# Rotating the three SBUF places of the FFN weight units in a hybrid decoder layer on eight cores

## The chip, the cores and the metric

The kernel runs on the eight cores of one Trainium2 chip. Every core takes half of the tokens of one of the four sequences, so all run the same program on data of their own. The metric is the device time of the slowest core, in microseconds (us). Engine names: PE is TensorE, DVE is VectorE, ACT is ScalarE, POOL is GpSimd, SP is SyncE.

## The reference

One decoder layer over `x` of 4 x 2048 x 2048 in float32. RMSNorm and one input projection feed two head groups: a causal pooling mixer and sparse attention with a compressed, a selected and a sliding-window branch. Their outputs pass an output projection and are added to `x`. Then follow the two steps that matter here, and a last RMSNorm:

```python
h = h + swiglu(rmsnorm(h, ffn_norm_g[i]), w_gate[i], w_up[i], w_down[i])
gate = jax.nn.sigmoid((rmsnorm(h, ple_norm_g[i]) @ w_ple_gate[i]).astype(jnp.float32)).astype(h.dtype)
h = h + (p[i] @ w_ple_proj[i]) * gate
...
def swiglu(x, w_gate, w_up, w_down):
    return (jax.nn.silu(x @ w_gate) * (x @ w_up)) @ w_down
```

The hidden width of the FFN is 5632, that is 44 chunks of 128.

## The kernel before, in words

**Order of the work.** The program is written as a list of operations, each with the buffers that it reads and writes (class `Sched`). Two buffers whose byte ranges in SBUF overlap depend on each other: the first use of the later one waits for all readers of the earlier one (`buf`, `_touch`, lines 54 to 83). A planner (`order`, lines 174 to 277) then plays the list through with a cost per operation and writes down, for each engine, the order in which its operations start. On the chip each engine runs its list in that order and waits on semaphores, so a wait holds up all that stands behind it on that engine. Of operations that are ready at the same planned time, the one that comes first in the program goes first. For DMAs the planner assumes 290e3 bytes per us (line 135), shared evenly by the bytes of a piece between the SP queue and the POOL queue when both hold work (`flow`, lines 207 to 229), each queue being first in, first out, with a start 1.2 us after its issue (line 264) and 0.55 us from landing to the reader (line 246).

**FFN.** Each core holds 1024 tokens as two halves of 512 (called half 0 and half 1). The 44 chunks are done in three groups of 16, 16 and 12 (`NQ_FF`, line 351). Gate and up weights come in *units* of 256 columns. The first pair of units is multiplied plainly (`plain_pair`); all others by a scheme with seven products of eight matmuls each instead of eight (`seven`, lines 191 to 227), for which DVE first forms sums of weight quarters (`weight_sums`, line 134). A unit needs 8 KB per partition for its weights and three sums of 2 KB. Three places take turns: unit `u` of the list `SEQ` uses place `u % 3` (lines 1129 to 1142). The down weights of the first two groups go through the same places as units 16 to 23 and 40 to 47. `SEQ` has 60 units; the last group is units 48 to 59, so unit 57 is in place 0, unit 58 (the last gate) in place 1, and unit 59 (the last up) in place 2.

**The last group's down projection.** Its down weights are eight tiles `wdn` of 6 KB each (line 1335), all in bytes of their own:

```python
wdn = [tile(f"wdl{i}", (R1 + 12 * KB, R1 + 18 * KB, R5 + 28 * KB, R5 + 34 * KB, R5, R5 + 6 * KB, R1, R1 + 6 * KB)[i], [12, 256], BF16) for i in range(8)]
...
    in_turn(latest + [load_dn(WD_FIRST[gi - 1])])
...
late = [load_dn(dmc) for dmc in range(2, 6)]
```

They are used in the order 6, 7, 0, 1, 2, 3, 4, 5 (`DM_LAST`, line 1330). Tiles 6, 7, 0 and 1 are loaded while the last group runs (line 1354). Tiles 2 to 5 (`late`, line 1358) lie in the region at `R5` where the units' places are, and so wait for units. Each load is three DMAs on the POOL queue that cast float32 to bfloat16. The embedding input `pT` (line 1360, two DMAs) lies at `AH` and waits for the unit that had that place. The first two gate weights of the next stage, `wpg0` and `wpg1`, come behind them (line 1378).

At the same time SP reads the residual stream back from HBM (`y_mid`) in 18 loads of 512 KB in one fixed order (lines 1367 to 1376). For most of half 1 it lies in two pieces, which DVE adds on arrival (line 1375, six additions of 1024 columns).

The products themselves are 32 tiles of 12 matmuls (lines 1381 to 1388), 16 for half 0 and then 16 for half 1. PSUM has 8 banks and the tiles take them in turn (`bank`), tile `k` and tile `k + 8` the same one; behind the first tile of half 1 the norm of half 0 takes a bank as well, which shifts the later ones by one. DVE adds each tile to the residual (`add_h`, line 963), and that frees the bank. The adds of L543 belong to the norm's statistics. Behind it comes the gate of the layer embedding (`ple`, line 1428; its own matmuls are L455 and L1440).

**At the start of the FFN**, units 0 to 2 are loaded into the places as soon as the output projection is done with the weights `wo` that lie there (lines 1156 and 1157).

The lines that the change touches, and those that use them:

```python
1108 UNITS = [([R5, R5 + 8 * KB, R5 + 10 * KB, R5 + 12 * KB]), [R5 + 14 * KB, R5 + 22 * KB, R5 + 24 * KB, R5 + 26 * KB], [R5 + 28 * KB, R5 + 36 * KB, R5 + 38 * KB, AH]]
1110 for i, o in enumerate(UNITS):
1111     w_ = view(o[0], [2, 8, 2, 128], BF16)
1112     B = S.buf(f"uw{i}", o[0], 8 * KB)
1113     units.append((w_, B, [tile(f"ut{i}{k}", o[1 + k], [8, 128], BF16) for k in range(3)]))
...
1131         w_, B, _ = units[u % 3]
1132         latest[:] = [load("pool", f"uw{u % 3}", w_.rearrange("p a b c d -> p (a b c d)"), SEQ[u], B)]
```

Of the kernel before, what the change touches and what calls it, by code (L numbers as in the profile page):

```python
# [15 lines left out]
KB = 1024  # L16
# [329 lines left out]
R4, R5, R6 = int(116.5 * KB), int(148.5 * KB), int(188.5 * KB)  # L346
# [6 lines left out]
def build():  # L353
# [43 lines left out]
    def view(off, shape, dtype=F32):  # L397
        n = int(np.prod(shape)) * (2 if dtype == BF16 else 4)
        assert off % 4 == 0 and n % 4 == 0 and off + n <= ARENA_BYTES, (off, shape)
        ap = arena[0:128, off // 4:(off + n) // 4]  # L400
        if dtype == BF16:
            ap = ap.bitcast(BF16)
        if len(shape) > 1:
            names = "abcd"[:len(shape)]
            kw = {names[i]: shape[i] for i in range(len(shape) - 1)}
            ap = ap.rearrange(f"p ({' '.join(names)}) -> p {' '.join(names)}", **kw)
        return ap
# [71 lines left out]
    AH = SCR + 12 * KB  # L479
# [625 lines left out]
        for q in range(4):  # L1105
            S.dma("sp", lambda e, q=q: e.dma_start(out=h_d[:, 4 * q:4 * q + 4, h, :], in_=hT[h][:, 4 * q:4 * q + 4, :]), f"hs{h}{q}", B_h[h][4 * q:4 * q + 4], [B_hd_of[4 * q + k][h] for k in range(4)])

    UNITS = [([R5, R5 + 8 * KB, R5 + 10 * KB, R5 + 12 * KB]), [R5 + 14 * KB, R5 + 22 * KB, R5 + 24 * KB, R5 + 26 * KB], [R5 + 28 * KB, R5 + 36 * KB, R5 + 38 * KB, AH]]
    units = []
    for i, o in enumerate(UNITS):  # L1110
        w_ = view(o[0], [2, 8, 2, 128], BF16)
# [526 lines left out]
```

How the kernel before makes its waits and increments, by code:

```python
        def run(e, engobj):  # L309
            waited = {}
            for o in ops[e]:
                need = {}
                for d in o.deps:
                    if d.dma_key is None:
                        sem, val, key = esem[d.eng], d.sigval, ("e", d.eng)
                    else:
                        sem, val, key = dsem[d.dma_key], d.dma_val, ("d", d.dma_key)
                    if need.get(key, (None, -1))[1] < val:
                        need[key] = (sem, val)
                for key, (sem, val) in need.items():
                    if waited.get(key, -1) >= val:
                        continue
                    waited[key] = val
                    engobj.wait_ge(sem, val)
                ins = o.fn(engobj)
                if o.dma_key is not None:
                    ins.then_inc(dsem[o.dma_key], 16)
                    for fn in o.more:
                        fn(engobj).then_inc(dsem[o.dma_key], 16)
                elif o.signal:
                    ins.then_inc(esem[e], 1)
```

## Time and profile before

| what | us |
|---|---|
| median of 3 runs | 1563.32 |
| lowest of the 3 runs | 1561.86 |
| the profiled execution's own time | 1561.98 |
| its span on the slowest core (core 1) | 1560.4 |
| spans of the eight cores | 1552.2 to 1560.4 |
| PE busy on core 1 | 1510.2 |

The span is from a core's first instruction to its last one. The execution's own time holds 1.6 us around it. A row of the trace names the line, the engine, the operation, out<-in and the count, and in brackets the idle time before it with what ended it.

### The profile page before, as it was taken

Reading aid. Unit: us, or ns where it says so; the run is one execution under the profiler, and the core shown is the slowest. Engines: PE = TensorE matmul, PEld = TensorE weight load, DVE = VectorE, ACT = ScalarE, POOL = GpSimd, SP = SyncE. Lnnn points to the kernel's source line nnn. Section 1 sums busy time; section 2 is a strip of 40 time slices with the busy share of each in tenths; the row PEclk is TensorE's granted clock in tenths of the full one; section 3 lists DMA queues with packets and bytes.
Section 4 is the critical chain, followed back from the end, with each engine's and each line's share of the span. In section 5 each row is a group of like instructions: output and inputs, shape, how many; then the busy total and the mean of one; then the engine's idle time right before and its main releaser. Section 6 shows DMA issues by size and latency. Waiting matters only on the chain.

```text
span 1560.4 us, 25895 instructions; the slowest of 8 cores (1552.2 to 1560.4 us)
## 1 busy us (share of the span) xinstructions
PE 1510.2 (97%) x8332; PEld 763.9 (49%) x8332; DVE 965.9 (62%) x1868; ACT 596.0 (38%) x1057; POOL 412.2 (26%) x570
## 2 busy tenths in 40 slices
PE   5899999999999999999999999999999999899996
PEld 1475564555554444444444444444444444344486
DVE  3686225888653467666666665867665564457766
ACT  4545327767673123322312223232222322124366
POOL 1322310100012101434334433444343443122030
PEclk9999999999999999999999999999999999899998
DMA  9955742311129943655599958778999675987023
GB/s 224 205 155 129 113 70 42 62 29 29 29 69 205 238 138 66 95 83 82 88 207 213 196 84 156 149 152 163 239 215 188 107 119 108 235 160 129 1 109 109
DMA packets 104724, 202.40 MB, mean 130 GB/s; under 512 B 12048, under 2 KB 17808, under 8 KB 104464
## 3 DMA queue, kind: packets, MB, share of 16 engines
q0 software_dynamic: 58320, 105.96, 44.5%
q1 hardware_dynamic: 46272, 94.79, 18.9%
q8 instruction: 69, 1.13, 0.3%
q14 instruction: 63, 0.52, 0.1%
HBM read 268.64 MB, written 36.70 MB: 196 GB/s over the span
## 4 chain that ended last, share of the span: by engine, by line
PE 90%; DMA 5%; DVE 1%; issue 1%; ACT 1%; POOL 0%; SPq 0%; DVEq 0%; ACTq 0%; POOLq 0%
PE ps L1200 44%; PE ps L455 36%; PE ps L1022 3%; PE ps L1014 3%; DMA arena<-wkv 2%; DMA arena<-y_mid 2%; PE ps L1016 1%; PE ps L1440 1%; PE ps L615 1%; DMA arena<-x 1%; DMA arena<-wgate 0%; PE ps L550 0%; POOL arena L435 0%; PE ps L1037 0%; PE ps L1031 0%
## 5 line engine op out<-in xcount | busy, mean ns | idle before, releaser
L1200 PE MATMUL ps<-arena 128*128 128x512 bf16 x3248 | 703.5, 380 | 4.4 <-ACT arena L1205 4.1
L455 PE MATMUL ps<-arena 128*128 128x512 bf16 (+6 forms) x3488 | 652.4, 338 | 11.3 <-DVE arena L963 6.5
L1200 PEld LDWEIGHTS ps<-arena 128*128 128x128 bf16 x3248 | 318.0, 98 | 389.8 <-issue 9.3
L455 PEld LDWEIGHTS ps<-arena 128*128 128x128 bf16 x3488 | 330.4, 98 | 283.0 <-issue 32.6
L1205 ACT ACTIVATE arena<-ps 128x512 f32<-128x512 f32 x232 | 138.2, 597 | 435.9 <-PE ps L1200 435.4
L1209 DVE TENSOR_TENSOR arena<-ps,arena 128x512 f32<-128x512 f32 x174 | 114.2, 684 | 190.3 <-PE ps L1200 183.6
L1209 POOL TENSOR_TENSOR arena<-arena 128x512 f32<-128x512 f32 x116 | 153.0, 1335 | 290.0 <-ACT arena L1205 290.0
L1017 ACT ACTIVATE arena<-ps 128x512 bf16<-128x512 f32 x216 | 121.0, 599 | 55.8 <-PE ps L1016 31.1
L542 ACT ACTIVATE arena<-arena 128x512 f32<-128x512 f32 x120 | 73.6, 625 | 165.2 <-DVE arena L963 138.5
L1139 DVE TENSOR_TENSOR arena<-arena 128x1024 bf16<-128x1024 bf16 x174 | 113.8, 693 | 22.5 <-DMA arena<-wdown 11.0
L543 DVE TENSOR_TENSOR arena<-arena 128x512 f32<-128x512 f32 x120 | 85.6, 714 | 48.4 <-ACT arena L542 43.7
L1141 DVE TENSOR_TENSOR arena<-arena 128x1024 bf16<-128x1024 bf16 x116 | 87.5, 754 | 9.1 <-DVE arena L1139 0.5
L435 POOL DMA_DIRECT2D arena<-wup x88 | 47.7, 556 | 143.6 <-PE ps L455 95.3
L1014 PE MATMUL ps<-arena 128*128 128x512 bf16 x216 | 78.2, 379 | 1.0 <-ACT arena L1032 0.4
L963 DVE TENSOR_TENSOR arena<-ps,arena 128x512 f32<-128x512 f32 x64 | 43.7, 687 | 51.1 <-PE ps L455 51.0
L565 DVE SCALAR_TENSOR_TENSOR arena<-arena 128x512 bf16<-128x512 f32 x96 | 64.1, 744 | 14.6 <-ACT arena L552 13.4
L1022 PE MATMUL ps<-arena 128*128 128x129 bf16 x864 | 70.4, 220 | 1.0 <-ACT arena L1017 1.0
L1022 PEld LDWEIGHTS ps<-arena 128*128 128x128 bf16 x864 | 56.3, 97 | 26.9 <-issue 18.1
L435 POOL DMA_DIRECT2D arena<-wgate x88 | 47.6, 558 | 72.4 <-PE ps L1200 41.6
L435 POOL DMA_DIRECT2D arena<-wdown x88 | 47.6, 564 | 40.6 <-PE ps L1200 34.9
L1264 ACT ACTIVATE arena<-arena 128x512 f32<-128x512 f32 x63 | 39.0, 630 | 46.9 <-DVE arena L1209 46.9
L615 PE MATMUL ps<-arena 128*128 128x512 bf16 x128 | 35.1, 431 | 19.1 <-DMA arena<-wkv 18.6
(146 smaller groups left out, 1053.1 us busy)
## 6 DMA issues: line engine op xcount, KB each, us to landing
arena<-x SPq DMA_DIRECT2D x48, 512.0 KB, 11.3
arena<-wup POOLq DMA_DIRECT2D x88, 256.0 KB, 7.8
arena<-wgate POOLq DMA_DIRECT2D x88, 256.0 KB, 7.7
arena<-wdown POOLq DMA_DIRECT2D x88, 256.0 KB, 9.0
arena<-y_mid SPq DMA_DIRECT2D x38, 512.0 KB, 9.3
y_mid<-arena SPq DMA_DIRECT2D x64, 256.0 KB, 6.4
arena<-wout POOLq DMA_DIRECT2D x32, 256.0 KB, 12.3
h_mid<-arena SPq DMA_DIRECT2D x8, 1024.0 KB, 19.9
```

Source lines behind the costliest of these rows:

```text
L435: fns = [lambda e, i=i: e.dma_start(out=dst[..., i * (n // k):(i + 1) * (n // k)], in_=src[..., i * (n // k):(i + 1) * (n // k)]) for i in ...
L455: PE(lambda e, i=i, lhsT=lhsT, rhs=rhs: e.matmul(out, lhsT=lhsT, rhs=rhs, start=(i == 0), stop=(i == n - 1)), reads(i), [PB[pb]])
L542: ACT(lambda e: e.activation(out=q, in_=src, func=AF.Square), [B_src], [Bq])
L543: DVE(lambda e: e.tensor_tensor(out=a, in0=a, in1=q, op=ALU.add), [Ba, Bq], [Ba])
L1014: PE(lambda e: e.matmul(four(ps[sb][:]), lhsT=kT_[:, g, pos(kt):pos(kt) + 128], rhs=q_of(g, ot), start=True, stop=(bias is None)), B_k + B ...
L1017: ACT(lambda e: e.activation(out=flat(p), in_=ps[sb][:], func=AF.Exp, scale=SCALE), [PB[sb]], [Bp])
L1022: PE(lambda e, r=r, bk=bk, c0=c0: e.matmul(ps[bk][:, c0:c0 + 129], lhsT=p[:, r, :], rhs=v1[:, vk, kt, 0:129], start=(first and r % 2 == 0) ...
L1139: DVE(lambda e, t=t, a=a, b=b: e.tensor_tensor(out=t, in0=P[a], in1=P[b], op=ALU.add), [B], [Bt])
L1141: DVE(lambda e, a=a, b=b: e.tensor_tensor(out=P[a], in0=P[a], in1=P[b], op=ALU.subtract), [B], [B])
L1200: PE(lambda e, dc=dc, r=r: e.matmul(ps[pb][:], lhsT=lhs[:, dc, :], rhs=r, start=(first and dc == 0), stop=(last and dc == 7), skip_group_c ...
L1205: ACT(lambda e: e.activation(out=t, in_=ps[pb][:], func=AF.Copy), [PB[pb]], [Bt])
L1209: eng(lambda e: e.tensor_tensor(out=out, in0=in0, in1=in1, op=op), r, w)
```

## The change

The three entries of `UNITS` are rotated by one. Nothing else is edited.

```diff
-    UNITS = [([R5, R5 + 8 * KB, R5 + 10 * KB, R5 + 12 * KB]), [R5 + 14 * KB, R5 + 22 * KB, R5 + 24 * KB, R5 + 26 * KB], [R5 + 28 * KB, R5 + 36 * KB, R5 + 38 * KB, AH]]
+    UNITS = [[R5 + 14 * KB, R5 + 22 * KB, R5 + 24 * KB, R5 + 26 * KB], [R5 + 28 * KB, R5 + 36 * KB, R5 + 38 * KB, AH], [R5, R5 + 8 * KB, R5 + 10 * KB, R5 + 12 * KB]]
```

By that the bytes from `R5` + 28 KB to 40 KB and `AH`, where down tiles 2 and 3 and `pT` are loaded, belong to place 1 (last used by unit 58) and no longer to place 2 (last used by unit 59). The bytes from `R5` to 14 KB, where down tiles 4 and 5 are loaded, belong to place 2 and no longer to place 0. The first units change as well: unit 0 takes the bytes that unit 1 had, unit 1 those of unit 2, unit 2 those of unit 0.

## Rows read from the trace of the kernel before

**Rows 1.** The page: chain by engine, and the line that PE waited at most.

```profile
PE 90%; DMA 5%; DVE 1%; issue 1%; ACT 1%; POOL 0%; SPq 0%; DVEq 0%; ACTq 0%; POOLq 0%
...
L455 PE MATMUL ps<-arena 128*128 128x512 bf16 (+6 forms) x3488 | 652.4, 338 | 11.3 <-DVE arena L963 6.5
```

**Rows 2.** PE in order of time around the last group's down projection: start, us, line.

```profile
1323.38 26.06 PE L455 MATMUL ps<-arena 128*128 128x512 bf16 x120
1352.32 5.28 PE L455 MATMUL ps<-arena 128*128 128x512 bf16 x12 [2.88 <-DVE arena L963]
1361.25 37.46 PE L455 MATMUL ps<-arena 128*128 128x512 bf16 x165 [3.65 <-DVE arena L963]
```

**Rows 3.** Stretches: length, busy per engine (instructions), PE's granted clock, DMA share, GB/s.

```profile
1311.30:1316.00 4.70, 4.70 (x23) 2.15 (x22) 0.69 (x1) 1.85 (x4) 0.00 (x0) 1.00 0.02 3
1316.00:1323.40 7.40, 7.40 (x36) 3.35 (x35) 2.77 (x5) 1.19 (x2) 3.47 (x4) 1.00 0.79 244
1336.00:1349.40 13.40, 13.40 (x63) 5.87 (x60) 5.46 (x9) 1.89 (x3) 0.00 (x0) 1.00 1.06 224
1349.40:1361.30 11.90, 5.37 (x14) 1.69 (x14) 5.62 (x8) 1.99 (x4) 0.00 (x0) 0.71 1.05 232
1361.30:1375.00 13.70, 13.70 (x56) 5.85 (x57) 6.33 (x8) 1.78 (x3) 4.24 (x8) 0.88 1.00 259
```

**Rows 4.** DVE in order of time in the same stretch.

```profile
1339.19 0.69 DVE L963 TENSOR_TENSOR arena<-ps,arena 128x512 f32<-128x512 f32 x1 [0.33 <-PE ps L455]
1345.40 1.23 DVE L1375 TENSOR_TENSOR arena<-arena 128x1024 f32<-128x1024 f32 x1 [5.52 <-DMA arena<-y_mid]
1351.49 0.68 DVE L963 TENSOR_TENSOR arena<-ps,arena 128x512 f32<-128x512 f32 x1
1356.43 1.23 DVE L1375 TENSOR_TENSOR arena<-arena 128x1024 f32<-128x1024 f32 x1 [4.25 <-DMA arena<-y_mid]
1360.42 0.68 DVE L963 TENSOR_TENSOR arena<-ps,arena 128x512 f32<-128x512 f32 x1
1363.40 1.23 DVE L1375 TENSOR_TENSOR arena<-arena 128x1024 f32<-128x1024 f32 x1 [2.30 <-DMA arena<-y_mid]
1402.82 10.69 DVE L565 SCALAR_TENSOR_TENSOR arena<-arena 128x512 bf16<-128x512 f32 x16 [1.81 <-ACT arena L552]
```

**Rows 5.** POOL in order of time: the queue of the weight loads.

```profile
1307.11 2.50 POOL L1209 TENSOR_TENSOR arena<-arena 128x512 f32<-128x512 f32 x2 [9.59 <-ACT arena L1205]
1322.42 1.12 POOL L435 DMA_DIRECT2D arena<-p  x2 [0.73 <-PE ps L1200]
1324.14 6.34 POOL L435 DMA_DIRECT2D arena<-wdown  x12 [0.60 <-PE ps L455]
1363.77 2.12 POOL L435 DMA_DIRECT2D arena<-wpg  x4 [33.28 <-DMA arena<-y_mid]
```

**Rows 6.** The 12 issues for `wdown` of 1324.1 to 1329.8: time to landing.

```profile
DMA to landing us min/median/max: 11.4/22.2/33.0
```

**Rows 7.** SP in order of time: the queue of the residual's loads.

```profile
1315.95 10.34 SPq L1371 DMA_DIRECT2D arena<-y_mid  x7
```

**Rows 8.** The page's DMA queues: packets, MB, share of 16 engines over the span.

```profile
q0 software_dynamic: 58320, 105.96, 44.5%
q1 hardware_dynamic: 46272, 94.79, 18.9%
```

**Rows 9.** POOL and DVE at the start of the FFN.

```profile
504.21 2.12 POOL L435 DMA_DIRECT2D arena<-wup  x4 [17.85 <-PE ps L455]
531.96 2.13 POOL L435 DMA_DIRECT2D arena<-wgate  x4 [4.97 <-PE ps L455]
...
565.59 10.69 DVE L565 SCALAR_TENSOR_TENSOR arena<-arena 128x512 bf16<-128x512 f32 x16 [0.90 <-ACT arena L552]
```

**Rows 10.** The chain that ended last, behind the second stall: start, us, what.

```profile
1398.70 0.86 PE ps L550 x2
1399.56 24.66 PE ps L455 x114
```

## The prediction

> **What bounds the kernel now.** I read the page first. PE holds 90% of the chain that ended last, and the one line at which PE idles for more than a few microseconds is L455: 11.3 us, of which 6.5 end with DVE's add at L963 [rows 1]. So a change can only win where PE stands still, or where it runs at its lower clock. PE in order of time shows both in one place, the last group's down projection [rows 2]. From 1323.38 it does 120 matmuls (ten product tiles, called tiles from here on; the weights are down tiles) in 26.06 us, 217 ns each. Then it idles 2.88 us, does one tile in 5.28 us (440 ns a matmul), idles 3.65 us, and does 165 more in 37.46 us. The stretches view has the granted clock: 1.00 up to 1349.4, a mean of 0.71 to 1361.3 and 0.88 to 1375, so PE fell to its lower level of 1.2 GHz behind each of the two stops [rows 3].
>
> What this place costs on core 1, against 217 ns a matmul:
> - idle: 2.88 + 3.65 = 6.53 us
> - the slow tile: 5.28 - 12 x 0.217 = 2.68 us
> - the rest of the slow clock: 37.46 - 165 x 0.217 = 1.66 us
>
> That is 10.9 us in all. Every core has a place like it.
>
> Why does PE stop? It restarts at 1352.32 and 1361.25, 0.15 us behind the ends of DVE's adds of 1351.49 and 1360.42 [rows 4]. The add of 1351.49 is the ninth of nine at L963 since the stage began, that of tile 9. An eleventh tile in program order would need the bank of tile 3, six adds earlier; the one that shares tile 9's bank is tile 17, the first of half 1. So the planner has put tile 17 at once behind tile 10, out of turn. Its arithmetic in the code shows why. With both queues full it gives each 145e3 bytes/us. POOL's queue has pT (1.05 MB) and down tiles 2 and 3 (1.57 MB each): 7.2 + 10.8 + 10.8 = 28.9 us from about 1324, so down tile 3 would land at 1353. The tile that needs it, the eleventh, is due at 1323.4 + 10 x 2.61 = 1349.5. It is not "ready", so the planner takes tile 17, whose bank has only just been filled. (I use this arithmetic for the order alone, never for a time of the chip.)
>
> DVE makes it worse: it stands at L1375 from 1339.9 to 1345.4 and from 1352.2 to 1356.4 for residual loads, and the adds queue behind [rows 4]. Those loads are late because the DMA engines are full: share 1.06 from 1336, against 0.02 from 1311.3 to 1316 [rows 3].
>
> **The change part by part.**
>
> *Down tiles 2, 3 and pT.* They wait for unit 58 instead of 59. A unit is seven products of eight matmuls, 56 x 0.216 = 12.1 us, so unit 58 ends at 1323.4 - 12.1 = 1311.3. pT's bytes come free two products (3.5 us) earlier, at 1307.8, and POOL is busy until 1309.6 [rows 5]. So pT issues at 1309.6 instead of 1322.42, and tiles 2 and 3 at about 1311.5 instead of 1324.14. Six issues at 0.53 us end at 1314.7, before POOL's next pair of adds, one unit (12.1 us) behind that of 1307.11; nothing else is queued there.
>
> *Down tiles 4 and 5* now wait for unit 59. They stood fourth and fifth in the queue and were issued behind its end anyway, at 1327 to 1330 [rows 5]. The cost is 0, or a gain of up to 3 us as six issues fewer stand before them; I take 0.
>
> *The transfers.* One POOL transfer takes 0.445 x 1560.4 / 404 = 1.72 us of all engines (105.96 MB in 0.262 MB pieces), one SP transfer 0.189 x 1560.4 / 181 = 1.63 us [rows 8]. From 1345.4 to 1356.4, with both queues full, SP landed two: 5.5 us each, a share of 0.30 [rows 4]. POOL's 14 need 24.1 us. I allow 1.7 us from issue to first data on both queues (an estimate, which shifts both alike): POOL's start at 1311.3 and run alone until SP's at about 1318 (issue 1315.95 [rows 7]): 6.7 us done. The other 17.4 at a share of 0.70 take 24.9 us, so down tile 5 lands at 1343. Before, it landed at 1329.8 + 33.0 = 1362.8 [rows 6]. SP has 4.6 transfers by then and goes on at 1.63. The first pair of half 1 (its 7th and 8th) lands at 1348.5, the second at 1352, the third at 1355; before 1345.4, 1356.4 and 1363.4 [rows 4].
>
> The Trainium skill has a rule that speaks against a gain here (Trainium Kernel Development and Optimization, Key Constraints): DMAs of all queues run on the same 16 engines and interleave, and several issuing queues save issue time alone. The trace agrees: SP's pace goes from 1.6 to 5.5 us. By this rule the first pair comes later, as worked out above, and the most to be won is the idle time of the engines that is now used; that is the second rival.
>
> *What the planner makes of it.* By its arithmetic down tiles 2 to 5 are now due at 1324, 1335, 1346 and 1357, and the tiles that need them at 1344, 1349, 1355 and 1360. All are ready in time, so half 0 goes in program order, and a tile needs the bank of one eight tiles (21 us) back. DVE's wait at L1375 then falls inside that cover: by the same arithmetic the first pair is due at about 1349, where it really lands. If that cover were gone, it would cost what it costs now.
>
> *What is late next.* PE then has 32 tiles x 2.61 = 83.4 us without a stop. The next consumer is the norm of half 0: its matmul L550 came at 1398.7 and its 16 scalings ended at 1413.5, 4.8 us before the gate stage [rows 4, 10]. In program order half 0's sum is done after 16 tiles, at 1365 plus 3 us, and the scalings near 1384, 23 us early. The loads of wpg wait for the residual's third pair, 1363.77 before [rows 5], about 1355 after, and are used from 1407 on. So the shift reaches the end of the chain, all PE from there [rows 10]. For waits of DVE that still show through (the last two pairs of half 1 share the engines with wpg) I take 0.7 us; bounds are 0 and the whole 10.9.
>
> *The start.* Unit 0 takes the issue slot of 504.21, units 2 and 1 the later ones, the last at 531.96. The normed input comes at 565.6 [rows 9], 33 us later, against four transfers of 1.72 us: no cost, and no gain, as nobody waits there. Were that cover gone, a wait for one unit would cost at most its four transfers, 6.9 us.
>
> *The 60 units between.* Each place serves 20 units before and after, so anything that hangs on an address is summed to the same total; 0, and no row shows an operation whose time depends on its address.
>
> **Sum.** Gain 10.9 - 0.7 = 10.2 us. The profiled execution took 1561.98 us, 1.6 above its span: 1561.98 - 10.2 = 1551.8. The median of the runs is 1.3 above the profiled one, so the forecast for the median is **1552 us**, own range 1549 to 1555.
>
> **The rivals.**
> 1. *Bound by the transfers* (the rule above): half 0 goes in order, yet PE still stops for residual or weights. For it: share above 1.0 for 25 us [rows 3]. Against: no tile in order meets a late landing above. What is won is engine time that lay idle, 1311.3 to 1318: 6.7 us, 1563.3 - 6.7 = 1556.6.
> 2. *It does not do what it says:* the rows name DVE, not a weight, at both stops [rows 2]. If tile 17 stands out of turn for another reason, PE waits as now: 1563.
> 3. *Slower.* The planner keeps tile 17 early, with DVE's first addition of a pair ahead of the adds of tiles 7 to 9, and that pair lands at 1348.5 instead of 1345.4. The first stop grows by 3.1 us, with 1.7 more at the lower clock; the second keeps its length: 1563.3 + 4.8 = 1568. It decides where the first pair lands behind 1345.4 with tile 17 still the eleventh.
>
> **How the numbers follow.** Forecast 0.72; rival 1 0.14; rival 2 0.08; rival 3 0.06. The range of 8 in 10 takes the forecast's and rival 1's and reaches up to the edge of rival 2: 1548 to 1562. 2% of 1563 is 31 us, about what a measurement of this kernel can tell from no change; no case comes near it. Faster by over 2%: 0.01; within: 0.97; slower by over 2%: 0.02, for a new order of the 60 units that stalls more than once.
>
> **What would show it.** Right: three groups of POOL issues (pT, then six for wdown) between 1309 and 1315; PE in one block of L455 from 1323 to about 1407, granted clock 1.00; the row "L455 waits for L963" gone; DVE's first L1375 at 1348 to 1350; L550 near 1368. Wrong: an idle row at L455 with a y_mid landing behind it (rival 1), the 12-matmul block still alone (2), or one later and longer (3).

## Result and profile after

| | before | after |
|---|---|---|
| median of the runs, us | 1562.87 | 1553.89 |
| the profiled execution, us | 1561.98 | 1552.73 |
| its span on the slowest core, us | 1560.4 (core 1) | 1551.2 (core 0) |

One of the four runs of each kernel was in a slower state (1716.57 and 1641.72 us), and the ratios and all times from here on leave such runs out; without it the medians are 1562.42 and 1552.73 us. The ratio is 0.9939 with a 95% interval of 0.9916 to 0.9961: a real gain, and one of 0.6%.

On the page of after, this is the chain that ended last by engine, and the line that PE had waited at most (columns as in [rows 1]).

```profile
PE 93%; DMA 3%; DVE 1%; issue 1%; ACT 1%; POOL 0%; DVEq 0%; ACTq 0%; POOLq 0%; SPq 0%
...
L455 PE MATMUL ps<-arena 128*128 128x512 bf16 (+7 forms) x3428 | 639.2, 336 | 7.2 <-DMA arena<-wkv 3.8
```

L455's idle time went from 11.3 to 7.2 us, and its first releaser is no longer the add of L963 but a load of another stage. PE in order of time on core 0 of after, to be held against [rows 2]:

```profile
1323.01 49.59 PE L455 MATMUL ps<-arena 128*128 128x512 bf16 x224
1374.19 1.10 PE L550 MATMUL ps<-arena 128*128 128x512 f32 x2 [1.60 <-DVE arena L543]
1375.12 37.07 PE L455 MATMUL ps<-arena 128*128 128x512 bf16 x168
...
1471.60 2.12 PE L455 MATMUL ps<-arena 128*128 128x288 bf16 x16
```

Both stops of [rows 2] are gone, and one of 1.60 us is new, at the norm of half 0. The other seven cores look like this one; the stop at L550 is 0 to 2.37 us long. The same stretches as in [rows 3], on core 0 of after:

```profile
1311.30:1316.00 4.70, 4.70 (x23) 2.13 (x22) 0.58 (x1) 1.82 (x3) 3.18 (x6) 1.00 0.75 94
1336.00:1349.40 13.40, 13.35 (x63) 6.09 (x63) 6.23 (x9) 3.15 (x5) 0.00 (x0) 1.00 0.99 229
1349.40:1361.30 11.90, 11.79 (x55) 5.42 (x56) 4.97 (x7) 1.26 (x2) 0.29 (x1) 1.00 0.99 333
1361.30:1375.00 13.70, 12.05 (x53) 5.27 (x54) 10.18 (x15) 3.41 (x6) 3.96 (x8) 1.00 1.04 232
```

The DMA engines now work at 0.75 in the first stretch, where they stood at 0.02, and PE's clock stays at 1.00 (its level of 2.4 GHz) all the way.

**Where the time came from.** The first matmul of 288 columns in the gate stage is a mark behind which all versions take about the same time (78.5 to 80.0 us to the end of the span, over all cores of all versions here). In front of it lies the same work each time, so the length from the last matmul of L1200 to this mark is called "the stage" below. Up to the gate stage's first matmul would not do as a measure: before has 11 more gate matmuls ahead of it (120 + 12 + 165 + 114 = 411 of L455 in [rows 2, 10], against 229 + 171 = 400 on core 1 of after). Before, the stage took 156.4 to 160.3 us over the eight cores; after, 146.6 to 149.2. The three cores with 146.6 have no stop at all in it, so 146.6 is what the matmuls alone need. On the two slowest cores it is 157.7 against 148.4: 9.3 us, which is the whole of the span's 1560.4 - 1551.2 = 9.2. On these two cores nothing was won or lost anywhere else.

DVE in order of time on core 0 of after, with the last of the first nine adds at L963 and then the additions of residual pairs (compare [rows 4]):

```profile
1346.59 0.69 DVE L963 TENSOR_TENSOR arena<-ps,arena 128x512 f32<-128x512 f32 x1 [0.33 <-PE ps L455]
1354.50 1.23 DVE L1375 TENSOR_TENSOR arena<-arena 128x1024 f32<-128x1024 f32 x1 [7.22 <-DMA arena<-y_mid]
...
1360.66 1.22 DVE L1375 TENSOR_TENSOR arena<-arena 128x1024 f32<-128x1024 f32 x1
...
1366.15 1.22 DVE L1375 TENSOR_TENSOR arena<-arena 128x1024 f32<-128x1024 f32 x1
```

This was foreseen only in part. DVE waits longer for the first pair than before (7.22 us against 5.52), and the pair comes 9 us later by the clock of the span (1354.50 against 1345.40). But PE does not notice. What differs is the place of the wait: nine adds now stand ahead of it on DVE, before it was six, and the adds of tiles 7, 8 and 9 stood behind it. The planner's own plan, followed through its code, says why. Counted from the end of the products, it has the first pair added at 17.0 us in before, between the adds of tiles 6 and 7; with the weights issued earlier it counts more bytes in front of the residual's loads and has the pair added at 24.2 us, behind the add of tile 9. That it is nine adds and not eight is chance: in the plan the pair is ready at 23.7 us, 0.1 us after the add of tile 9 has started. (These are planned times; on the chip the pair was added at 22.0 us before, 1345.40 - 1323.38, and at 31.5 us after, 1354.50 - 1323.01.) POOL's queue on core 0 of after, to be held against [rows 5]:

```profile
1309.96 1.11 POOL L435 DMA_DIRECT2D arena<-p  x2 [0.72 <-PE ps L1200]
1311.69 3.18 POOL L435 DMA_DIRECT2D arena<-wdown  x6 [0.61 <-PE ps L1200]
1323.78 3.23 POOL L435 DMA_DIRECT2D arena<-wdown  x6 [2.46 <-PE ps L455]
```

The change has done what it says: pT and down tiles 2 and 3 are issued 12.5 us earlier by the clock of the span, which is one unit. Tiles 4 and 5 gain 3.1 us: their first issue came 3.88 us behind the products' end before (the seventh of 12) and comes 0.77 us behind it now. One edit has had three effects: the loads run earlier, the planner puts half 0's tiles in program order, and it puts DVE's first pair behind nine adds. The experiments take these apart, though not every combination was run.

### The profile page after: what moved, and what is told of

Same layout as the page of the kernel before. It is cut to its first block, busy times and chain, and to the rows that moved or that the text cites. A ratio compares the mean times of both kernels' runs of the same rounds, so it can differ in the third digit from the quotient of the medians.

```text
span 1551.2 us, 25767 instructions; the slowest of 8 cores (1542.2 to 1551.2 us)
## 1 busy us (share of the span) xinstructions
PE 1496.9 (96%) x8192; PEld 762.8 (49%) x8332; DVE 962.4 (62%) x1868; ACT 593.9 (38%) x1055; POOL 414.0 (27%) x570
## 4 chain that ended last, share of the span: by engine, by line
PE 93%; DMA 3%; DVE 1%; issue 1%; ACT 1%; POOL 0%; DVEq 0%; ACTq 0%; POOLq 0%; SPq 0%
PE ps L1200 45%; PE ps L455 38%; PE ps L1022 3%; PE ps L1014 3%; DMA arena<-wkv 2%; PE ps L1016 1%; PE ps L1440 1%; PE ps L615 1%; DMA arena<-x 1%; PE ps L550 0%; PE ps L1037 0%; DVE arena L1209 0%; PE ps L1031 0%; PE ps L1060 0%; DVE arena L1478 0%
## 5 line engine op out<-in xcount | busy, mean ns | idle before, releaser
L1200 PE MATMUL ps<-arena 128*128 128x512 bf16 x3183 | 698.4, 379 | 8.4 <-ACT arena L1205 4.2
L455 PE MATMUL ps<-arena 128*128 128x512 bf16 (+7 forms) x3428 | 639.2, 336 | 7.2 <-DMA arena<-wkv 3.8
L1200 PEld LDWEIGHTS ps<-arena 128*128 128x128 bf16 x3248 | 317.5, 98 | 389.1 <-issue 7.6
L455 PEld LDWEIGHTS ps<-arena 128*128 128x128 bf16 x3488 | 329.5, 98 | 271.5 <-issue 17.9
L1139 DVE TENSOR_TENSOR arena<-arena 128x1024 bf16<-128x1024 bf16 x174 | 113.1, 690 | 24.6 <-DMA arena<-wdown 15.3
L1141 DVE TENSOR_TENSOR arena<-arena 128x1024 bf16<-128x1024 bf16 x116 | 84.1, 725 | 9.0 <-DVE arena L1139 0.5
L963 DVE TENSOR_TENSOR arena<-ps,arena 128x512 f32<-128x512 f32 x64 | 43.5, 687 | 42.7 <-PE ps L455 42.6
```

Source lines behind the costliest of these rows:

```text
L455: PE(lambda e, i=i, lhsT=lhsT, rhs=rhs: e.matmul(out, lhsT=lhsT, rhs=rhs, start=(i == 0), stop=(i == n - 1)), reads(i), [PB[pb]])
L1139: DVE(lambda e, t=t, a=a, b=b: e.tensor_tensor(out=t, in0=P[a], in1=P[b], op=ALU.add), [B], [Bt])
L1141: DVE(lambda e, a=a, b=b: e.tensor_tensor(out=P[a], in0=P[a], in1=P[b], op=ALU.subtract), [B], [B])
L1200: PE(lambda e, dc=dc, r=r: e.matmul(ps[pb][:], lhsT=lhs[:, dc, :], rhs=r, start=(first and dc == 0), stop=(last and dc == 7), skip_group_c ...
```

## Experiments

In all of them `.behind = op` sets the planner's order of two operations on one engine; it adds no wait on the chip. The places of tiles and adds are those of the planner's order, with which the counts of matmuls and adds in the traces agree. `n_op` and `n_add` are the length of the list of operations ahead of the call. All versions compute the whole reference. Each ratio is to runs of before that were taken beside that version. The stage is given as the median core and the range over cores, from the profiled execution.

| version | loads | place of tile 17 | adds ahead of the first pair | ratio to before | stage, us |
|---|---|---|---|---|---|
| before | late | 11th | 6 | 1 | 157.7 (156.4 to 160.3) |
| loads_late | late | 11th | 6 | 0.9997 [0.9985, 1.0009] | 158.3 (155.3 to 160.2) |
| pt_last | weights two transfers earlier | 13th | 5 | 1.001 [0.9999, 1.0022] | 160.2 (158.8 to 162.9) |
| half1_held | late | in turn | 6 | 1.005 [1.003, 1.007] | 166.9 (165.2 to 171.5) |
| pairs_held | late | 11th | all of half 0 | 0.9967 [0.9949, 0.9986] | 149.4 (148.8 to 154.4) |
| after | early | in turn | 9 | 0.9939 [0.9916, 0.9961] | 147.9 (146.6 to 149.2) |
| 17_early | early | 11th | 9 | 0.9939 [0.9917, 0.9961] | 146.6 (146.6 to 148.2) |
| 17_and_pairs_early | early | 11th | 6 | 1.0016 [1.0001, 1.003] | 156.2 (149.9 to 161.4) |
| other_way | earlier still | in turn | 8 | 0.9928 [0.9911, 0.9946] | 147.5 (146.6 to 149.3) |
| after_pairs_held | early | in turn | all of half 0 | 0.9927 [0.9905, 0.9949] | 146.6 (146.6 to 149.1) |

**Is the earlier issue all that the rotation does?** The rotated places, but pT and down tiles 2 and 3 made to wait for unit 59's last output as they did before:

```diff
-            return load("pool", f"wdn{dmc}", flat(w_), wd_d[fq * 8 + dmc, :, 0:ncq * 256], Bw)
+            return load("pool", f"wdn{dmc}", flat(w_), wd_d[fq * 8 + dmc, :, 0:ncq * 256], Bw, [B_hf[11][1]] if dmc in (2, 3) else [])
...
-            load("pool", "pT", flat(pT), p_d, B_pT)
+            late[0].behind = load("pool", "pT", flat(pT), p_d, B_pT, [B_hf[11][1]])
```

> The changed kernel with its rotated places, but pT and down tiles 2 and 3 wait for an output of the last unit, so they are issued near 1325 as before. If the earlier issue is all that the rotation does (both theories): the two stops of 3 to 4 us near 1349 and 1357 are back and the time is that of the kernel before, 1560 to 1565 us. If the rotation gained by something else (other addresses, the order of the first loads): 1552 to 1556 us.

Measured: 0.9997 [0.9985, 1.0009], 1562.74 us. PE on its core 0:

```profile
1325.01 26.06 PE L455 MATMUL ps<-arena 128*128 128x512 bf16 x120
1357.37 4.25 PE L455 MATMUL ps<-arena 128*128 128x512 bf16 x12 [6.29 <-DVE arena L963]
1362.56 36.20 PE L455 MATMUL ps<-arena 128*128 128x512 bf16 x167 [0.94 <-DVE arena L963]
```

It is the picture of before again: 120 matmuls, a stop, 12 alone, a stop. So the whole gain hangs on the earlier issue; the new addresses of the 60 units are worth nothing that the runs tell apart (the interval is 1.5 us to either side), as the prediction had it.

**A little earlier only.** Before, with pT put behind the down tiles in POOL's queue, so that the weights come pT's share earlier:

```diff
-            load("pool", "pT", flat(pT), p_d, B_pT)
+            load("pool", "pT", flat(pT), p_d, B_pT).behind = late[3]
```

> The kernel before with one edit: pT is issued behind down tile 5 instead of ahead of down tile 2, so all four down tiles land 3.4 us earlier at no change of places. The planner then puts tile 17 two tiles later, behind tile 12, and DVE's second pair ahead of the add of tile 9. Theory A: that add still waits for a pair that lands near 31 us behind the last unit, so PE stops again when it comes to tile 17; 1557 to 1564 us. Theory B: the weights come earlier and the pairs later, total traffic is the same, 1561 to 1565. If a late down tile 3 were all that mattered: 1552 to 1555.

Measured: 1.001 [0.9999, 1.0022], 1565.78 us. The waits of PE on its core 1 (line, releaser: us in total, times, longest):

```profile
PE ps L455 <- DVE arena L963: 9.8, 4, 4.7
PE ps L455 <- ACT arena L551: 1.1, 1, 1.1
```

PE still stops for adds, four times now. Tile 17 has moved to the 13th place, since the weights come two transfers earlier. But POOL's queue as a whole starts no earlier, and the planner has the first pair even earlier, at 14.7 us, with five adds ahead of it. On this core the first piece of the down weights landed 9.8 us behind the products' end and the last 38.0, against 12.1 and 39.4 on core 1 of before. Weights earlier by that much win nothing.

**Tile order alone.** Before, with every tile of half 1 put behind the last of half 0:

```diff
+                    n_op = len(S.ops)
...
+                    if h == 0:
+                        last_mm = S.ops[-1]
+                    else:
+                        S.ops[n_op].behind = last_mm
```

> The kernel before, places as they were, but the first matmul of each tile of half 1 is held behind the last tile of half 0, so that PE goes in program order though the down weights still land late. Theory A (PE lost its time because tile 17 stood out of turn behind tile 10, with its partner's add stuck on DVE): PE stops only for the landings of down tiles 4 and 5, due at 1354.7 and 1359.9 and landed near 1356.4 and 1362.8 before, about 3 us instead of 10.9; 1553 to 1557 us. Theory B (the loss is the traffic itself, and only an earlier start of the loads takes it away): 1559 us or more, with idle time at L455 of 5 us or more.

Measured: 1.005 [1.003, 1.007], 1571.14 us: slower than before. PE in order of time on its core 1:

```profile
1325.13 31.51 PE L455 MATMUL ps<-arena 128*128 128x512 bf16 x144
1358.71 5.34 PE L455 MATMUL ps<-arena 128*128 128x512 bf16 x24 [2.07 <-DMA arena<-wdown]
1365.76 13.11 PE L455 MATMUL ps<-arena 128*128 128x512 bf16 x60 [1.71 <-DMA arena<-wdown]
...
1394.25 2.04 PE L550 MATMUL ps<-arena 128*128 128x512 f32 x2 [15.38 <-DVE arena L543]
```

The stops for adds are gone and the two for down tiles are short, 3.8 us together. What made it slower was new: 15.38 us at the norm, whose sum waits for DVE. DVE of the same core shows why:

```profile
1349.67 1.23 DVE L1375 TENSOR_TENSOR arena<-arena 128x1024 f32<-128x1024 f32 x1 [8.04 <-DMA arena<-y_mid]
...
1380.65 1.23 DVE L1375 TENSOR_TENSOR arena<-arena 128x1024 f32<-128x1024 f32 x1 [5.67 <-DMA arena<-y_mid]
...
1388.58 1.23 DVE L1375 TENSOR_TENSOR arena<-arena 128x1024 f32<-128x1024 f32 x1 [4.46 <-DMA arena<-y_mid]
```

The first pair again has six adds ahead of it, and all six pairs stand among half 0's adds; the last one ends at 1389.8, and behind it half 0's last sums. So the tile order alone is not the cause: with the loads late and six adds ahead of the pair, putting it right only moves the damage from the bank to the norm. Neither theory had this, and the expected time was missed; the next run holds the pairs and not the tiles.

**DVE's order alone.** Before, with the six additions of pairs put behind the add of half 0's last tile, and the tiles left as they were:

```diff
-                    DVE(lambda e, h=h, c=c, y=y: ..., B_h[h][c] + [By], B_h[h][c])
+                    pairs.append(DVE(lambda e, h=h, c=c, y=y: ..., B_h[h][c] + [By], B_h[h][c]))
...
+                    if h == 0 and dm == DM_LAST[-1]:
+                        for o in pairs:
+                            o.behind = S.ops[n_op]
```

> The kernel before, places and order of the tiles as they were (tile 17 still behind tile 10), but DVE's six additions at L1375 are held behind the add of tile 16, so that no add of half 0 stands behind a residual load. Theory A: the add of tile 9 comes at 1347.5 instead of 1351.5, so PE does not stop at tile 17, nor behind it; idle at L455 under 2 us, 1551 to 1556 us. Theory B: the loads land no earlier, so 1559 us or more. If the order of the tiles alone made the loss, 1560 to 1564.

Measured: 0.9967 [0.9949, 0.9986], 1559.21 us. PE on its core 3, whose stage is the longest:

```profile
1323.94 28.65 PE L455 MATMUL ps<-arena 128*128 128x512 bf16 x132
1353.54 34.48 PE L455 MATMUL ps<-arena 128*128 128x512 bf16 x159 [0.95 <-DVE arena L963]
...
1396.50 24.99 PE L455 MATMUL ps<-arena 128*128 128x512 bf16 x102 [3.74 <-ACT arena L551]
```

With no weight there earlier (the last piece of tile 5 landed 39.9 us behind the products' end on this core, 39.4 on core 1 of before) and tile 17 still out of turn, the first stop is gone and the second shrinks to 0.95 us. So it was DVE's standing at L1375 ahead of the adds that stopped PE. But the ratio shows only about half of the gain, 0.33% of 0.61%. What is missing lies behind the norm, with a new wait of 3.74 us for ACT's L551 on this core and 6.8 us at a granted clock of 0.50 around it: half 0 ends late (its L550 comes at 1387.86, 63.9 us behind the products' end, against 51.2 in after), and the norm has no room before the gate stage. On the median core the stage is 157.7 - 149.4 = 8.3 us shorter, on the longest 160.3 - 154.4 = 5.9. Whether tiles in turn would bring the rest with late loads is not shown: the pairs held and the tiles in turn, with the loads late, was not run.

**After, with tile 17 early again.** The first matmuls of tiles 11 to 16 put behind tile 17:

```diff
+                    if h == 0:
+                        firsts.append(S.ops[n_op])
+                    if h == 1 and dm == DM_LAST[0]:
+                        for o in firsts[10:]:
+                            o.behind = S.ops[-1]
```

> The changed kernel, loads early, but tiles 11 to 16 are held behind tile 17, so that tile 17 again stands behind tile 10. Theory A: DVE now does nine adds before its first wait at L1375, the add of tile 9 among them, so tile 17 finds its bank free; within 3 us of the changed kernel, 1551 to 1556. If the order of the tiles alone made the loss: a stop of 3 us or more near 1349 and a granted clock of 0.5 behind it, 1559 to 1563.

Measured: 0.9939 [0.9917, 0.9961], 1552.99 us, as after. PE and then DVE of its core 3:

```profile
1323.17 51.96 PE L455 MATMUL ps<-arena 128*128 128x512 bf16 x240
1376.46 1.10 PE L550 MATMUL ps<-arena 128*128 128x512 f32 x2 [1.33 <-DVE arena L543]
```

```profile
1346.82 0.69 DVE L963 TENSOR_TENSOR arena<-ps,arena 128x512 f32<-128x512 f32 x1 [0.39 <-PE ps L455]
1356.20 1.23 DVE L1375 TENSOR_TENSOR arena<-arena 128x1024 f32<-128x1024 f32 x1 [8.70 <-DMA arena<-y_mid]
```

The eleventh tile takes tile 9's bank at once, and PE runs 240 matmuls without a stop, since the add of tile 9 is done at 1347.5 with the pair behind it, not ahead. With nine adds ahead of the pair, the tile that the prediction blamed costs nothing that the runs tell apart. One thing is not as in before: there the planner's list has four matmuls of tile 24 right behind tile 17, in the same bank, so that the second stop of before is a wait for tile 17's own add; here tile 24 stands in turn. The run before this one still has it early, and its 0.95 us are what it costs with the pairs held.

**After, with tile 17 and the pairs early.** The same, and the adds of tiles 7 to 9 put behind the first pair and that of tile 10 behind the second:

```diff
+                    if h == 0 and dm in DM_LAST[6:10]:
+                        S.ops[n_add].behind = pairs[dm == DM_LAST[9]]
```

> The changed kernel with tile 17 behind tile 10 (as in e3) and, in addition, DVE's first addition at L1375 ahead of the adds of tiles 7 to 9 and the second ahead of that of tile 10, as DVE had them in the kernel before; the loads stay early. Theory A: both conditions of the loss are back, and the first pair now lands at 25 to 32 us, so tile 17 waits for the add of tile 9 until about 30 to 37 us behind the last unit; a stop of 4 to 11 us with the lower clock behind it, stage 96 to 104 us, 1560 to 1568 us. If earlier loads were what counts by themselves: stage 87 to 90, 1551 to 1556.

Measured: 1.0016 [1.0001, 1.003], 1566.26 us. PE and DVE of its core 0:

```profile
1320.97 26.06 PE L455 MATMUL ps<-arena 128*128 128x512 bf16 x120
1356.41 31.30 PE L455 MATMUL ps<-arena 128*128 128x512 bf16 x120 [9.38 <-DVE arena L963]
```

```profile
1353.25 1.22 DVE L1375 TENSOR_TENSOR arena<-arena 128x1024 f32<-128x1024 f32 x1 [14.13 <-DMA arena<-y_mid]
1354.39 1.88 DVE L963 TENSOR_TENSOR arena<-ps,arena 128x512 f32<-128x512 f32 x3
```

With the loads as early as in after, this order alone takes the whole gain back. DVE stands 14.13 us, three adds run behind the pair, and PE restarts when they are done. Against the run before it differs in DVE's order only.

**Two versions that might be better.** First the places rotated the other way, so that pT and all four late down tiles fall to places that are free yet another unit earlier:

```diff
+    UNITS = [[R5 + 28 * KB, R5 + 36 * KB, R5 + 38 * KB, AH], [R5, R5 + 8 * KB, R5 + 10 * KB, R5 + 12 * KB], [R5 + 14 * KB, R5 + 22 * KB, R5 + 24 * KB, R5 + 26 * KB]]
```

> The three places rotated the other way: down tiles 2, 3 and pT lie in the place of unit 57, down tiles 4 and 5 in that of unit 58, so every one of them is issued one unit (12 us) earlier than in the changed kernel and before the residual loads begin. Theory A: the pairs of half 1 land at 13 to 20 us behind the last unit instead of 25 to 32, DVE stands at none of them for long, and the wait of 0 to 2.8 us at the norm's matmul goes; the stage takes 87.2 us on all eight cores, 1549 to 1553 us, at most 3 us below the changed kernel. Theory B (the traffic bounds the stage): more is won, 6 us or more, 1545 or less.

Measured: 0.9928 [0.9911, 0.9946], 1552.72 us. POOL on its core 1, and its DVE's first pair:

```profile
1296.84 1.12 POOL L435 DMA_DIRECT2D arena<-p  x2 [0.72 <-PE ps L1200]
1298.56 3.18 POOL L435 DMA_DIRECT2D arena<-wdown  x6 [0.61 <-PE ps L1200]
1310.65 3.23 POOL L435 DMA_DIRECT2D arena<-wdown  x6 [2.45 <-PE ps L1200]
```

```profile
1343.57 1.22 DVE L1375 TENSOR_TENSOR arena<-arena 128x1024 f32<-128x1024 f32 x1
```

Here the first pair is there before DVE comes to it, 21.6 us behind the products' end (1321.97 on this core); in after it is 25.4 to 32.3 us over the cores. No core has a stop of PE in the stage. And yet the interval overlaps that of after: loads one unit earlier are worth nothing that these runs tell apart. All they had left to win was the stop of 0 to 2.37 us at the norm, and on some cores a lower clock took part of that back (last section). After, with the six pairs held behind half 0's adds (the edit of the run on DVE's order):

> The changed kernel with DVE's six additions at L1375 held behind the add of tile 16. Theory A: what is left of the loss in the changed kernel (0 to 2.8 us at the norm's matmul) comes from DVE standing at the first of these additions, so it goes, if the additions that now stand close together before the norm do not cost as much; stage 87.2 to 89 us on all cores, 1549 to 1554 us. Theory B: no difference to the changed kernel in the stage's spread over the cores.

Measured: 0.9927 [0.9905, 0.9949], 1552.98 us. Five cores have a stage of 146.6 us, the value without a stop, and a sixth 146.9; one core keeps a stop of 1.6 us for an add. Its interval too overlaps that of after, so neither is shown to be the better one.

## Why the prediction came out right, and where its reason was short

- **The number.** 1551.8 us for the profiled execution came close to the measured 1552.73. The forecast for the median does not follow from the sum: 1551.8 and the 1.3 us by which the median lay above it make 1553.1, not 1552. Measured were the two medians given with the result, 1553.89 and 1552.73. The 2% named as what a measurement can tell is too coarse as well: this interval reaches 0.2% to either side.
- **The place and the size of the loss: right.** 10.9 us were counted on core 1; its stage was 157.7 against 146.6 without a stop, 11.1.
- **What the change does: right.** pT at 1309.96 (said 1309.6), down tiles 2 and 3 at 1311.69 (1311.5), tiles 4 and 5 3.1 us earlier against the products' end (0 taken, up to 3 allowed). Start and the 60 units between: nothing that the run with the loads late can tell apart.
- **The transfers: mis-sized.** On core 0 of after, for pT's two pieces the time from issue to landing was

```profile
DMA to landing us min/median/max: 6.2/6.9/7.6
```

so the second, issued at 1310.5, was there at 1318.2 and not at 1314.7, as the working gives it (1311.3 + 2 x 1.72). No run shows the allowance of 1.7 us from issue to first data "on both queues". In the packet trace of this core POOL's first packet starts 1.3 us behind its issue, but the engines fill slowly (share 0.25, 0.64 and 0.96 in the three stretches of 2 us from 1310 on); SP's first packet starts 3.6 us behind its issue of 1315.58, beside POOL's, where it was 1.0 us in before. Over the cores pT's first piece took 3.4 to 6.3 us, so the worked 3.4 holds for the quickest. For the six weight pieces issued last, from 1323.78 on, it was

```profile
DMA to landing us min/median/max: 10.9/16.2/25.0
```

which puts down tile 5's last, issued near 1326.4, at 1351.4, not at 1343. The third of POOL's 14 pieces was already 3 us late and the 13th no later than that (1343.4); the last alone came 8 us behind the 13th. The first pair was added at 1354.50 on core 0 and not near 1348.5; over the cores, 25.4 to 32.3 us behind the products' end, where the prediction had 25.1. Of the sum only the 0.7 us hung on this.
- **The planner's order: right in both halves, but the wrong half was given the weight.** The sentence "So the planner has put tile 17 at once behind tile 10, out of turn" was taken for the cause, with DVE's wait as what "makes it worse". The runs turn this round. Tile 17 early costs nothing where nine adds stand ahead of the pair (0.9939), and in turn it is no cure where six do (1.005). Six adds ahead, with tile 17 the 11th, stop PE, with late loads (1, 0.9997) and with early ones (1.0016). Holding the pairs alone, with late loads, takes the first stop away and leaves 0.95 us of the second (0.9967). The sentence nearest to the real cause was a later one: "by the same arithmetic the first pair is due at about 1349, where it really lands", so that the wait "falls inside that cover". It stood there as a detail, and its time is near the plan's 24.2 us (1323.4 + 24.2 = 1347.6). That before's plan had the pair at 17.0 us, 5 us ahead of the chip, was not looked at. So the size came out right in part by luck: the one edit put both orders right, and the 10.9 us go whichever of them is blamed.
- **What is left: mis-sized.** 0.7 us were taken for waits that still show; on the slowest core it was 1.60 at L550, and its stage is 148.4 - 146.6 = 1.8 above the least. That is why the profiled execution gained 9.25 us (1561.98 - 1552.73) and not 10.2. The norm came 51.2 us behind the products' end (1374.19 - 1323.01), where 44.6 was said (1368 - 1323.4): the pairs that land later hold half 0's sum, since the stop at half 0's L550 is gone on all cores where they are held behind half 0's adds (after_pairs_held) or land earlier (other_way). Of the signs that were to show the forecast right, the two that name the pair (1348 to 1350) and L550 (near 1368) were missed on this core; the issues, the block of PE with its clock, and the row of L963 came as said.
- **Rival 1, bound by the transfers (the prediction once calls it the second): fell.** The DMA share stays near 1.0 from 1336 on, and the pair is added later, 25.4 to 32.3 us behind the products' end over the cores against 21.2 to 25.3 before, as the rule of the Trainium skill (Trainium Kernel Development and Optimization, Key Constraints: all queues share the same 16 engines and interleave) would have it; in this the trace agrees, with a wait of 7.22 us against 5.52. But of PE's waits only the stop at the norm hangs on it, and other_way, with the pair at 21.6 us, is not shown to be faster.
- **Rival 2 fell with the rows of POOL. Rival 3 did not come about, but its mechanism is real.** Made by hand in 17_and_pairs_early, it stopped PE for 9.38 us on core 0 and cost 0.16% against before (0.01% to 0.3%), some 2.5 us where 4.8 had been worked out. Its condition was put wrongly: what decides is not where the pair lands, but whether DVE's wait stands ahead of the adds of tiles 7 to 9. In after and 17_early the pair lands far behind 1345.4, and no product tile of PE stops for it.

What stays open: whether other_way or after_pairs_held beats after by a tenth of a per cent, and how the second half of the gain is shared between the tile order and the earlier landing of the weights.

## What to carry to other kernels

When a change moves a load, look at what its new due time does to the order on the other engines, not only at when the bytes land: here the loads were never awaited by PE, and the gain hung on three adds that no longer stood behind a wait on an in-order engine. Moving them alone brought about half of it, and putting them back took all of it away. For a stop that ends with engine X, ask what stood ahead of the releasing instruction on X, and try that order by itself before blaming the instruction that waits. Measure a stage between two marks with the same work between them: up to the gate's first matmul the gain would have looked 2.4 us larger here (11 matmuls of 0.217 us).

## What the runs showed of the hardware that was not expected

In some runs PE had stretches at a granted clock between its levels of 1.2 and 2.4 GHz, in other_way without having been idle. These are rows of the same stretch on core 0 and then on core 2 of other_way (columns as in [rows 3]):

```profile
1390.00:1406.00 16.00, 16.00 (x63) 6.69 (x62) 7.84 (x12) 3.38 (x6) 2.59 (x5) 0.82 0.59 94
```

```profile
1390.00:1406.00 16.00, 15.95 (x75) 7.25 (x75) 7.52 (x11) 4.79 (x8) 6.33 (x12) 1.00 0.74 128
```

Both were busy throughout, and core 0 did 63 matmuls where core 2 did 75. The trace's record of the granted clock reads 0.81 for 15.2 us on cores 0 and 1 and for 5 us on cores 4 to 7, and 1.00 on cores 2 and 3. It costs core 0 149.3 - 146.6 = 2.7 us of its stage, and is why other_way's median core has 147.5 and not 146.6. In every profile that has such stretches, both cores of a pair (0 and 1, 2 and 3, 4 and 5, 6 and 7) have them within half a microsecond of each other, each by its own time. In their stages they also stand in half1_held (all cores, 7 to 15 us each), loads_late (cores 2, 3, 6 and 7) and 17_and_pairs_early (cores 0 and 1), so up to 2.9 us of these stages (15.2 x 0.19) are not owed to the order; the profiles of before, after and 17_early show none. The cause was not tried.

The other surprise is how little it mattered that the DMA engines were full: in after their share is 0.99 to 1.04 from 1336 to 1375, PE's clock is 1.00, and core 1 does 229 matmuls in 49.59 us, 217 ns each, the pace that before had where it did not stop.
